# A four-layer hybrid decoder on eight cores: another order of the first loads, and the norms' squares added in a tree of two levels

## The reference, cut to what matters

```
def rmsnorm(x, g):
    y = xf * lax.rsqrt(jnp.mean(xf * xf, axis=-1, keepdims=True) + EPS)
    return y * g
...
for l in range(DEPTH):
    h = h + hybrid_mixer(rmsnorm(h, norm_mix[l]), ...)       # attention with decay (8 heads x 64), gated short conv, merge, w_o
    h = h + memory_attention(rmsnorm(h, norm_mem_q[l]), ...) # 4 heads x 128 over 256 memory tokens
    h = h + swiglu(rmsnorm(h, norm_ffn[l]), ...)             # 1024 -> 2 x 2816 -> 1024
```

## Time and profile before

| | |
|---|---|
| median of 3 runs | 4433.89 us (lowest 4430.71) |
| profiled execution, own time | 4430.21 us |
| its span on the slowest core | 4428.7 us (cores 4421.9 to 4428.7) |
| mean granted TensorE clock | 0.993 to 0.994 of full on every core |
| instructions | 70242, of them 21976 matmuls |

### The profile page before, as it was taken

One profiled execution on the slowest core, in us unless ns is written; L12 is line 12 of the kernel. 1 busy time (PEld: TensorE's weight loads), 2 busy tenths in 40 slices (PEclk: granted clock), 3 DMA queues, 4 the chain that ended last, 5 costly groups with the idle time before them and its releaser, 6 DMA issues.

```text
span 4428.7 us, 70242 instructions; the slowest of 8 cores (4421.9 to 4428.7 us)
## 1 busy us (share of the span) xinstructions
PE 4329.1 (98%) x21976; PEld 2042.0 (46%) x21976; DVE 2233.6 (50%) x3629; ACT 2707.8 (61%) x4731; POOL 758.1 (17%) x1672
## 2 busy tenths in 40 slices
PE   6988999999999999999999999999999999999999
PEld 3433444445444444444544444444454444444444
DVE  5555344565536633457544653446654555435544
ACT  5857756557556577655754667756566457764542
POOL 1211111112211111111211111111121111111111
PEclk9999999999999999999999999999999999999999
DMA  5542335443554423544455433354446543344554
GB/s 133 115 77 43 58 48 83 75 70 71 98 85 75 75 46 58 78 70 75 80 94 85 69 61 56 61 80 70 70 81 96 79 74 63 50 67 73 109 77 93
DMA packets 185524, 334.00 MB, mean 75 GB/s; under 512 B 22032, under 2 KB 49680, under 8 KB 184784
## 3 DMA queue, kind: packets, MB, share of 16 engines
q0 software_dynamic: 157248, 281.87, 41.5%
q1 hardware_dynamic: 27632, 47.40, 3.4%
q10 hardware_dynamic: 288, 0.23, 0.0%
HBM read 590.12 MB, written 21.30 MB: 138 GB/s over the span
## 4 chain that ended last, share of the span: by engine, by line
PE 94%; ACT 2%; issue 1%; DVE 1%; DMA 1%; SPq 0%; POOL 0%; ACTq 0%; DVEq 0%; POOLq 0%
PE ps L147 94%; ACT f L147 1%; ACT pt L147 1%; DVE RB L147 0%; DVE f L147 0%; DMA hT<-x 0%; SPq L147 0%; DMA RB<-aug 0%; DMA RB<-wp 0%; DVE uT L147 0%; ACT RB L147 0%; DMA aug<-f 0%; POOL pt L147 0%; ACT sq L147 0%; ACTq L146 0%
## 5 line engine op out<-in xcount | busy, mean ns | idle before, releaser
L147 PE MATMUL ps<-uT,RB 128*128 128x512 bf16 x10752 | 2459.5, 379 | 16.6 <-ACT pt L147 10.8
L147 PE MATMUL ps<-RB 128*128 128x512 bf16 (+5 forms) x7168 | 1693.9, 367 | 15.0 <-DMA RB<-aug 5.3
L147 PEld LDWEIGHTS ps<-uT,RB 128*128 128x128 bf16 x10752 | 1045.3, 98 | 1266.5 <-issue 43.8
L147 POOL DMA_DIRECT2D RB<-wp x1088 | 578.1, 533 | 2972.8 <-PE ps L147 2929.6
L147 PEld LDWEIGHTS ps<-RB 128*128 128x128 bf16 (+1 forms) x7168 | 690.0, 98 | 804.2 <-issue 43.7
L147 DVE TENSOR_TENSOR f<-ps,f 128x512 f32<-128x512 f32 x672 | 459.0, 690 | 1131.1 <-ACT f L147 819.4
L147 ACT ACTIVATE f<-ps 128x512 f32<-128x512 f32 (+1 forms) x864 | 511.6, 593 | 831.1 <-PE ps L147 823.2
L147 ACT ACTIVATE pt<-ps 128x512 bf16<-128x512 f32 (+1 forms) x1280 | 640.2, 578 | 149.8 <-PE ps L147 146.8
L147 ACT ACTIVATE f<-f 128x512 f32<-128x512 f32 (+2 forms) x1057 | 661.8, 626 | 99.4 <-ACT f L147 3.4
L147 DVE TENSOR_TENSOR hT<-ps,hT 128x512 f32<-128x512 f32 x640 | 430.9, 689 | 362.9 <-PE ps L147 361.3
L147 DVE TENSOR_TENSOR RB<-ps,f 128x512 bf16<-128x512 f32 (+1 forms) x608 | 417.1, 689 | 342.5 <-ACT f L147 204.6
(11 more groups left out here) (40 smaller groups left out, 949.7 us busy)
## 6 DMA issues: line engine op xcount, KB each, us to landing
RB<-wp POOLq DMA_DIRECT2D x960, 256.0 KB, 4.3
RB<-wp POOLq DMA_DIRECT2D x128, 224.0 KB, 4.0
out<-hT SPq DMA_DIRECT2D x32, 256.0 KB, 2.6
hT<-x SPq DMA_DIRECT2D x3, 2048.0 KB, 11.3
kvs<-RB SPq DMA_DIRECT2D x32, 192.0 KB
RB<-kvs SPq DMA_DIRECT2D x32, 192.0 KB
kvs<-RB SPq DMA_DIRECT2D x32, 140.0 KB
RB<-kvs SPq DMA_DIRECT2D x32, 140.0 KB
```

The source lines that it names most:

```text
L147: ins = getattr(eng, o.fn[0])(**o.fn[1])
```

## The change

Constants of the planner get other values, and `LEVELS` and `AHEAD_PR` are new. The mixer's stream may hold ten panels (`first`) until the output projection of half (0, 0) is done, six after that. The six panels of head pair 0 of half (0, 1) stand ahead of the CQ panels of half (0, 0) in the order of loads. The FFN's stream starts at ("wo", (0, 0)) and not at ("mrg", (0, 0)). `norm_T` squares one block at a time, adds pairs and then pairs of pairs on VectorE, and has one product for four blocks, so two per norm. Its bank is taken at the first product; `nts` lets at most two norms run at once. At the start the ones (`aug<-ones`) go in two DMAs from ScalarE's queue instead of eight from SP's, an activation of one column follows the constants, and the first load on POOL's queue, wf, waits for x0's second piece and not for its first.

```diff
+LEVELS = 2
-PACE = {0: 0.707, (1, 1): 0.707}
-AHEAD = 2.99
-SLACK = 0.002
-ADJ = {'wo': -1.0, 'n3': -0.64, 'conv': 2.81, 's': -1.74, 'n2': 1.3, 'f': 0.64, 'ma': -1.85, 'n1': -0.92, ...}
-NS = 1.67
+PACE = {0: 0.733, (1, 1): 0.757, (2, 1): 0.71, (0, 0): 0.727, (1, 0): 0.741, (0, 1): 0.775, (2, 0): 0.756}
+AHEAD = 1.34
+SLACK = 0.0
+ADJ = {'wo': 0.6, 'n3': -1.5, 'conv': 3.03, 's': -1.38, 'n2': 1.3, 'f': 0.8, 'ma': -4.83, 'n1': 1.29, ...}
+NS = 1.37
+AHEAD_PR = 1
...
+                self.first = 10
...
-                if len(self.mine) >= self.most:
+                if len(self.mine) >= (self.most if ("wo", (0, 0)) in fired else self.first):
...
-            return [(key, p, 2048) for p in seq]
+            seq = [(key, p, 2048) for p in seq]
+            n = 6 * AHEAD_PR
+            if key == (0, 1):
+                seq = seq[n:]
+            if key == (0, 0):
+                i = [p for _, p, _ in seq].index(P_CQ)
+                seq[i:i] = [((0, 1), p + pr, 2048) for pr in range(AHEAD_PR) for p in (P_K, P_Q, P_V, P_GC, P_Z, P_GB)]
+            return seq
...
         def norm_T(l, tb, gbase, ev, name):
             bank = None
-            for k in range(0, 8, 2):
-                sqs = []
-                for i in range(2):
-                    yield U("act", ev=ev, rd=[H[k + i][tb]], take=[(sqp, 1)] + ([(banks, 1)] if k + i == 0 else []))
-                    if k + i == 0:
+            sums = []
+            for k in range(8):
+                yield U("act", ev=ev, rd=[H[k][tb]], take=[(sqp, 1)] + ([(nts, 1)] if k == 0 else []))
+                if k == 0:
+                    tok = nts.get()
+                sq = sqp.get()
+                A("act", "activation", [H[k][tb]], [sq], out=sq.ap[:, :], in_=H[k][tb].ap, func=AF.Square)
+                sums.append((0, sq))
+                while len(sums) > 1 and sums[-1][0] == sums[-2][0] < LEVELS:
+                    n, b = sums.pop()
+                    _, a = sums.pop()
+                    yield U("dve", rd=[a, b])
+                    A("dve", "tensor_tensor", [a, b], [a], n=256, out=a.ap[:, :], in0=a.ap[:, :], in1=b.ap[:, :], op=ALU.add)
+                    sqp.put(b)
+                    sums.append((n + 1, a))
+                if sums[-1][0] == LEVELS:
+                    n, a = sums.pop()
+                    yield U("pe", rd=[a], take=[(banks, 1)] if k < 2 ** LEVELS else [])
+                    if k < 2 ** LEVELS:
                         bank = banks.get()
-                    sqs.append(sqp.get())
-                    A("act", "activation", [H[k + i][tb]], [sqs[i]], out=sqs[i].ap[:, :], in_=H[k + i][tb].ap, func=AF.Square)
-                yield U("dve", rd=sqs)
-                A("dve", "tensor_tensor", sqs, [sqs[0]], n=256, out=sqs[0].ap[:, :], in0=sqs[0].ap[:, :], in1=sqs[1].ap[:, :], op=ALU.add)
-                sqp.put(sqs[1])
-                yield U("pe", rd=[sqs[0]])
-                mm(bank, bank.ap[:, :], ONESD, sqs[0].ap[:, :], k == 0, k == 6, [sqs[0], r_const])
-                sqp.put(sqs[0])
+                    mm(bank, bank.ap[:, :], ONESD, a.ap[:, :], k < 2 ** LEVELS, k == 7, [a, r_const])
+                    sqp.put(a)
+            nts.put(tok)
             yield U("act", rd=[bank], take=[(f32p, 1)])
...
-        for tb in range(4):
-            for kq in range(2):
-                DMA("sp", "ao", [], [x for y in r_ag for x in y], mb=0.01, out=ag_d[tb, kq][:, 3 * kq:3 * kq + 3, :], in_=one_d[2 * tb + kq])
         DMA("act", "cp", [], [r_pv2], mb=0.05, out=pv[:, :], in_=pv_d[:, :])
+        for kq in range(2):
+            DMA("act", "ao", [], [x for y in r_ag for x in y], mb=0.04, out=ag_d[:, kq, :, 3 * kq:3 * kq + 3, :].rearrange("t h r n -> t h (r n)"),
+                in_=one_d[4 * kq:4 * kq + 4].rearrange("t h r n -> t h (r n)"))
         for k in range(0, 8, 2):
-            DMA("sp", f"x0_{k}", [], [H[k][0], H[k + 1][0]], mb=0.25, out=hT[:, 0, k:k + 2, :], in_=x_d[:, 0, k:k + 2, :])
+            DMA("sp", f"x0_{k}", [], [H[k][0], H[k + 1][0]], mb=0.5, out=hT[:, 0, k:k + 2, :], in_=x_d[:, 0, k:k + 2, :])
...
-                DMA("sp", f"x{tb}", [last], [H[k][tb] for k in range(8)], mb=1.0, out=hT[:, tb, :, :], in_=x_d[:, tb, :, :])
+                DMA("sp", f"x{tb}", [last], [H[k][tb] for k in range(8)], mb=2.0, out=hT[:, tb, :, :], in_=x_d[:, tb, :, :])
...
+        A("act", "activation", [r_pv2], [r_pv2], n=1, out=pv2[:, 14:15], in_=pv2[:, 12:13], func=AF.Square)
-        DMA("pool", "wf", [H[1][0]], [r_wfr], mb=0.3, out=wfr[:, :, :], in_=wf_d[0])
+        DMA("pool", "wf", [H[3][0]], [r_wfr], mb=0.3, out=wfr[:, :, :], in_=wf_d[0])
...
-        spawn(ring([x for key in keys for x in ffn_panels(key)], streams[1], [("mrg", (0, 0))]), -1, "fring")
+        spawn(ring([x for key in keys for x in ffn_panels(key)], streams[1], [("wo", (0, 0))]), -1, "fring")
```

More of the change, by code:

```diff
@@ L326 @@
 GR = 512
+LEVELS = 2
 FFN_US = 226.0
 MIX_US = (290.0, 345.0)
-PACE = {0: 0.707, (1, 1): 0.707}
-AHEAD = 2.99
-SLACK = 0.002
-ADJ = {'wo': -1.0, 'n3': -0.64, 'conv': 2.81, 's': -1.74, 'n2': 1.3, 'f': 0.64, 'ma': -1.85, 'n1': -0.92, ('qkv', (3, 1)): -2.44, ('merge', (0, 0)): 0.87, ('merge', (1, 1)): -0.17, ('pv', (1, 1)): -0.63, ('wo', (1, 1)): -0.53, ('qkv', (2, 1)): -1.32, ('fin', (0, 0)): -1.58, ('n1', (0, 1)): -0.98, ('qkv', (0, 0)): 1.15, ('n3', (0, 0)): 0.35, ('pv', (2, 0)): -0.97}
-NS = 1.67
+PACE = {0: 0.733, (1, 1): 0.757, (2, 1): 0.71, (0, 0): 0.727, (1, 0): 0.741, (0, 1): 0.775, (2, 0): 0.756}
+AHEAD = 1.34
+SLACK = 0.0
+ADJ = {'wo': 0.6, 'n3': -1.5, 'conv': 3.03, 's': -1.38, 'n2': 1.3, 'f': 0.8, 'ma': -4.83, 'n1': 1.29, ('qkv', (3, 1)): -2.44, ('merge', (0, 0)): 0.87, ('merge', (1, 1)): -0.17, ('pv', (1, 1)): -0.63, ('wo', (1, 1)): -0.53, ('qkv', (2, 1)): -1.32, ('fin', (0, 0)): -1.58, ('n1', (0, 1)): -0.98, ('qkv', (0, 0)): 1.67, ('n3', (0, 0)): 0.35, ('pv', (2, 0)): 0.25, 'kv': 1.26, ('pv', (3, 1)): -1.69, ('fin', (2, 1)): -0.19, ('n1', (1, 0)): 1.68, ('kv', (3, 1)): 1.22, ('mem', (1, 0)): 0.36, ('pv', (1, 0)): 0.65, ('pv', (2, 1)): -1.45, ('ma', (2, 1)): -2.06, ('s', (3, 0)): 0.56, 'pv': -0.45, ('s', (0, 1)): -1.09, ('conv', (3, 0)): 2.64, ('ma', (0, 0)): -3.76, ('pv', (0, 1)): 1.0, ('kv', (0, 1)): 2.76, ('wo', (3, 1)): 1.01}
+NS = 1.37
+AHEAD_PR = 1
 KV_AT = (2, 3, 4, 5)
@@ L643, in ffn_panels, with __init__, get, put @@
             return seq
+        class Slots:
+            def __init__(self, n):
+                self.free = list(range(n))
+            def get(self):
+                return self.free.pop(0)
+            def put(self, x):
+                self.free.append(x)
+            def t_avail(self):
+                return 0.0
+        nts = Slots(2)
         def norm_T(l, tb, gbase, ev, name):
             bank = None
-            for k in range(0, 8, 2):
-                sqs = []
-                for i in range(2):
-                    yield U("act", ev=ev, rd=[H[k + i][tb]], take=[(sqp, 1)] + ([(banks, 1)] if k + i == 0 else []))
-                    if k + i == 0:
-                        bank = banks.get()
-                    sqs.append(sqp.get())
-                    A("act", "activation", [H[k + i][tb]], [sqs[i]], out=sqs[i].ap[:, :], in_=H[k + i][tb].ap, func=AF.Square)
-                yield U("dve", rd=sqs)
-                A("dve", "tensor_tensor", sqs, [sqs[0]], n=256, out=sqs[0].ap[:, :], in0=sqs[0].ap[:, :], in1=sqs[1].ap[:, :], op=ALU.add)
-                sqp.put(sqs[1])
-                yield U("pe", rd=[sqs[0]])
-                mm(bank, bank.ap[:, :], ONESD, sqs[0].ap[:, :], k == 0, k == 6, [sqs[0], r_const])
-                sqp.put(sqs[0])
@@ L1098, in mem_kv @@
             fire("kvm", l)
[L1100 to L1111, removed]
         pbs, qms, mas = Slots(2), Slots(4), Slots(4)
```

## The result

The changed kernel takes 4404.99 us by the median of its runs, 0.9936 of before with a 95% interval of 0.9907 to 0.9965. Run again later beside the kernel before (e8) it gave 0.9932 [0.9914, 0.9950]. That is 29 us less; 49 were forecast. The executions of the changed kernel that count lie between 4400.0 and 4406.4 us, so a difference of 2 or 3 us between two kernels is at the edge of what these runs tell.

The account below looks back on a forecast made before the run. TensorE, busy 98% of the span, was taken to bound the kernel. Products 19, start 6, panels 5 and hole 20, less 1 for adds, gave 49 us off 4430.2: 4381 us, range 4345 to 4415.

Parts of the forecast that it names:

- the place of the idle time: Seven tenths of TensorE's 99.6 us idle lie in the first tenth of the run, in layer 0.
- Step 1, the products: In the 48 norms, 96 fewer ones-matmuls at 0.2151 us: 20.6 us of TensorE work, 19 us off the path.
- Step 5, the reordering: Pace, priorities and planned load costs reorder everything after 410 us: taken as 0, at most 13 us won.
- Rival (b): Ends slower: FFN work spent earlier is missing as cover under memory attention, at worst 68 us, 4449 us; chance 0.08.
- Step 1, the adds: Two more VectorE adds per norm, 40 us in all, mostly hidden under TensorE: a cost of 1 us.
- The upper bound of 22 us: Most that the added adds could cost: 48 norms x 0.45 us, if every norm were exposed.
- Step 2, the start: First loads: x0 issued 5.4 us earlier, table load pulled ahead, first projection at 18.6 us: 6 us won, bounds 4.9 and 7.5.
- my lower bound of 4.9: Least gain from the first loads: the first square moving from 12.65 to about 7.8 us.
- Step 3, ten panels early: Until the first output projection, head pair 1's K, Q, V fill idle time in 24:60: 5 us, bounds 0 and 12.
- more than 29 that I named as a sign: The profile after would show more than 29 us of TensorE work in the window 24:60.
- Step 4, the hole: At 306 to 330 us, half (0,1)'s early panels fill TensorE's wait and keep full clock: 20 us of a possible 36.

Follow-up runs that it names:

- e8: The changed kernel run again, unchanged, beside the kernel before: 4404.4 us, 0.9932 of before.
- e1: Kernel before with only the new norms (adds of pairs, then pairs of pairs, two products a norm), old planner values: 4446.8 us, 1.0036 of before.
- e9: Kernel before with only the planner's new values: 4468.4 us, 1.0080 of before.
- e6: Changed kernel in its own order, first product of each norm written three times (96 more matmuls): 4423.3 us, one execution.
- e14: Kernel before in its own order, every second product of the norms left out, no adds added: 4417.3 us, 0.9967 of before.
- e4: Changed kernel with the planner's old values (pace, AHEAD, SLACK, ADJ, NS): 4437.4 us, 1.0021 of before.
- e13: Kernel before in its own order, four products a norm kept, one more VectorE operation before every second product: 4445.0 us, 1.0027 of before.
- e5: Kernel before in its own order, with two levels of adds and two products a norm: 4432.8 us, 1.0000 of before.
- e17: Changed kernel in its own order, the ones again as eight DMAs on SP before x0: 4407.5 us, 0.9944 of before.
- e7: Changed kernel in its own order, the one-column square reading a column of its own instead of waiting for pvec: 4405.4 us, 0.9937 of before.
- e11: Changed kernel with the old panels (six slots from the start, old load order, old FFN stream start): 4434.2 us, 1.0003 of before.
- e3: Kernel before with only the new panels (ten slots, new load order, new FFN stream start), old planner values: 4425.2 us, 0.9985 of before.
- e18: Changed kernel with 0.01 taken from every PACE: 4408.6 us, 0.9947 of before.

## Why the prediction was right or wrong

**The sign, the place of the idle time and the bound** were right, and 4405 lies in the range; the size was 29 us instead of 49.

Busy and idle time alone hide a part of the account. A matmul of 512 columns is drawn 379 ns long and the next usually starts 216 ns after it, so a wait of up to 163 ns counts as busy, and so does the longer step at a granted clock of 0.50. The starts of TensorE's matmuls and the granted clock give three sums: the usual steps, what steps took beyond the usual, up to as much again, in stretches at the lower of the two levels (0.50), and the rest, which is waits. Mean of six cores, us:

| | usual steps | lower clock | waits to 410 us | waits after |
|---|---|---|---|---|
| before | 4273.8 | 17.0 | 84.5 | 48.4 |
| changed kernel | 4253.1 | 11.9 | 64.2 | 64.6 |
| e1 tree | 4253.1 | 21.6 | 85.9 | 77.3 |
| e9 values alone | 4273.8 | 25.2 | 85.1 | 74.6 |

So the 30 us between the two kernels' last matmuls are 20.7 us of products, 5.1 of clock and 20.3 of waits won in the first 410 us, less 16.2 us of waits given back after that.

**Step 1, the products** (-19 us) was right: 18.9 us in e6, 14 to 15 in e14, whose order was not made for it.

**Step 5, the reordering, is the step that failed in the changed kernel**, "I take 0, bounds +13 won". It cost 11.5 us of idle time after 410 us, 16.2 us by the mean of six cores with the waits that busy time hides. That is the largest part of the 20 us by which the gain fell short. Rival (b) named the right loser, cover missing in attention's stages, and put it down to the pace alone. But e1, with the old pace, shows it too. With the old values the idle time there rose by 25 to 28 us (e1, e4), and the new values in the old kernel cost 36 us of time (e9). The values were not a step with a price of its own, as my sum had it; what they are worth depends on the parts beside them, so a sum of parts had no row for it.

**Step 1, the adds, failed as a mechanism.** "Where other work covers the norm, the 0.45 us costs nothing ... So I take 1 us." In the order of before they cost 12 to 13 us (e13), and with the products gone nothing is left of the tree's gain (e5, 1.0000). I looked at what TensorE waited for before the change. I did not look at the product, which stands first in TensorE's in-order queue until the longer line of adds is through, whatever work is ready behind it. The upper bound of 22 us held. In the changed kernel the adds show no wait; what part of its new order's loss is the price of making room for them, no run tells.

**Step 2, the start** (6 us): 4.3 us at the first projection on the slowest cores, 1.0 to 1.5 over all cores, 3 to 4 at the end (e17). Below my lower bound of 4.9. That bound was the first square's, forecast at 7.8; it came at 11.62 and not at 12.65, 1.0 us earlier, since the table load waited for pvec. pvec landing that late was not foreseen; e7 shows that it costs no time, since x0's last piece is what counts.

**Step 3, ten panels early** (5 us): idle time of 24:180 fell by 1.6 us, and 24:60 holds 27.97 us of work and not the more than 29 that I named as a sign. TensorE still waits 4.36 us for the second block's sums near 42 us, after 2.69 before. By these rows it was over-sized. Taken out of the changed kernel together with the fill of the hole, the panels bring back 7.8 us of idle time there (e11); alone in the old kernel they won none there (e3, 17.6 us after 17.0). The 16 and 32 matmuls of this step are 5.4 us and not 5.2.

**Step 4, the hole** (20 us): idle time of 300:410 fell by 15.1 us and the clock there is 0.95 instead of 0.86. With the clock's part the changed kernel gets 20 us more work done in that window, as forecast. But 8 us of it came back by 450 us. The mechanism was right.

**Settled by the traces:** e5's busy time fell by 7.6 us only while 20.7 us of matmuls went. On the two profiled cores 7.7 us more from the lower clock, all in the first 700 us, and 5.5 us more of short waits hidden under drawn matmuls fill it. By the mean of six cores e5 has 19.3 us more waits than before and 3.8 more of clock.

**Open:** no kernel tried here beats the changed one by more than the scatter; which orders do was not searched. Why an order costs what it costs was followed only to the waits for exponentials, not to the planner's choice.

## What to carry to other kernels

Where a planner writes every engine's order, price an edit twice: by its work in a fixed order, and by what a new order may cost, which here was 5 us (e18) to 36 us (e9) against parts worth 3 to 20. Keep the order and hide the edit from the planner's clock to measure the first. And an instruction added to an in-order queue that is half idle isn't free: ask who reads its result, and what stands behind that reader on the engine that bounds. Compare times of the first microseconds over all cores: here they differ by 4.6 us between the cores of one execution.

## What the runs showed of the hardware that was not expected

A small transfer issued at 1.5 us (pvec, 98 KB) was there at 3.9 to 5.3 us on the eight cores of before, where only small ones ran beside it. In the changed kernel, where 2 MB of x were issued from 1.07 on, it was there at 8.8 to 11.1. 96 VectorE operations of 0.42 us on an engine 50% busy lengthened the program by 12 to 13 us (e13): some 11 us of waits of TensorE, after 410 us all of them before sums of squares, and some 2 us of clock.
